# A hybrid mixer and sparse expert block: expert weights split in units per block, down product in f16, block columns copied by GpSimd

## The reference

```python
p_sel, g_sel = lax.top_k(p_group, 1)                 # group of a token
top_logits, top_idx = lax.top_k(sel_logits, TOP_K)   # two experts in it
gates = (p_sel * jax.nn.softmax(top_logits, axis=-1)).reshape(-1)
...
def expert_block(args):
    xb, e = args
    h = jax.nn.silu(xb @ w_gate[e]) * (xb @ w_up[e])  # w_gate, w_up: 1024 x 256
    return h @ w_down[e]                              # w_down: 256 x 1024
...
out = jnp.zeros((n + 1, d)).at[buf_tok].add(y * buf_gate[:, None])[:n]
```

## Time and profile before

| | us |
|---|---|
| median of 3 runs (lowest, highest) | 3261.25 (3260.13, 3263.42) |
| profiled execution, its own time | 3270.86 |
| its span, first to last instruction | 3269.3 |
| busy: PE, DVE, ACT, POOL | 3003.3, 2566.0, 2012.5, 949.9 |
| mean granted TensorE clock | 0.965 |

### The profile page before, as it was taken

The page is one execution under the profiler, slowest core; times in us unless marked ns, Lnnn a source line. Parts: engine busy times, 40 slices in busy tenths (PEclk is TensorE's granted clock), DMA queues, the critical chain, the costliest instruction groups (busy, mean ns, idle before and its releaser), DMA issues. The chain is left out here.

```text
span 3269.3 us, 82047 instructions
## 1 busy us (share of the span) xinstructions
PE 3003.3 (92%) x28810; PEld 2246.0 (69%) x28811; DVE 2566.0 (78%) x7193; ACT 2012.5 (62%) x4458; POOL 949.9 (29%) x994
## 2 busy tenths in 40 slices
PE   4878999999999999999999999997699999999970
PEld 4767878878887888788888878884344455554530
DVE  6678778887887888788878878886777888888755
ACT  7455566656565656665666656553566677777646
POOL 4213122212221322222122213222344444444420
PEclk9889999999999999999999999998899999999985
DMA  7010111121112121112112121115387777777749
GB/s 270 21 53 14 47 66 68 65 76 63 66 66 72 60 73 66 66 64 68 66 66 72 64 75 60 69 57 206 117 248 217 233 206 214 192 219 217 221 99 393
DMA packets 117811, 380.30 MB, mean 116 GB/s; under 512 B 18560, under 2 KB 18688, under 8 KB 105216
## 3 DMA queue, kind: packets, MB, share of 16 engines
q1 hardware_dynamic: 82528, 269.96, 22.8%
q0 software_dynamic: 29216, 89.30, 11.9%
q10 hardware_dynamic: 5760, 16.85, 1.3%
HBM read 280.05 MB, written 96.01 MB: 115 GB/s over the span
## 5 line engine op out<-in xcount | busy, mean ns | idle before, releaser
L597 PE MATMUL pj<-uT,W 128*128 128x128 f16 x15840 | 982.7, 220 | 8.1 <-POOL W L1732 8.1
L597 PEld LDWEIGHTS pj<-uT,W 128*128 128x128 f16 x15840 | 936.3, 98 | 54.1 <-issue 43.5
L2078 DVE SCALAR_TENSOR_TENSOR W<-W,ecol 128x512 f16<-128x512 f16 x664 | 447.4, 746 | 111.4 <-ACT W L2022 108.7
L2022 ACT ACTIVATE W<-W,ecol 128x512 f16 x664 | 415.8, 708 | 79.6 <-issue 77.3
L1986 PE MATMUL bA<-W,uT 128*128 128x512 f16 x1992 | 446.6, 381 | 5.4 <-issue 4.1
L1986 PEld LDWEIGHTS bA<-W,uT 128*128 128x128 f16 x1992 | 193.4, 98 | 229.0 <-issue 9.9
L1970 PE MATMUL pj<-W,qs 128*128 x664 | 303.3, 600 | 3.7 <-issue 2.8
L1781 POOL TENSOR_TENSOR dec<-tri,g 128x512 f32<-128x512 f32 x33 | 34.3, 1039 | 925.8 <-DVE g L1501 925.8
L953 ACT ACTIVATE ht<-ht 128x512 f32<-128x512 f32 x256 | 159.7, 625 | 87.5 <-DMA ht<-w_up 83.1
L1970 PEld LDWEIGHTS pj<-W,qs 128*128 128x128 f32 x664 | 121.4, 193 | 126.6 <-issue 126.3
L983 ACT ACTIVATE qh<-bA 128x256 f32<-128x256 f32 x198 | 76.6, 387 | 193.7 <-PE bA L697 189.7
(11 more groups left out here) (462 smaller groups left out, 6328.7 us busy)
## 6 DMA issues: line engine op xcount, KB each, us to landing
ht<-w_gate SPq DMA_DIRECT2D x128, 256.0 KB, 3.1
ht<-w_up SPq DMA_DIRECT2D x128, 256.0 KB, 3.3
W<-w_gate SPq DMA_DIRECT2D x32, 1024.0 KB
W<-w_up SPq DMA_DIRECT2D x32, 1024.0 KB
W<-w_down SPq DMA_DIRECT2D x32, 1024.0 KB
x_in<-xm SPq DMA_DIRECT2D x33, 512.0 KB, 4.4
ht<-xm SPq DMA_DIRECT2D x32, 512.0 KB, 3.5
h_rows<-ht SPq DMA_DIRECT2D x32, 512.0 KB
```

Of the source, the lines that this page charges most:

```text
L597: mm = pe.matmul(pj[g % 2][:, j, :], w16[:, k, w_half(w_high, COL[GROUPS[g]], 512, j * P, P)], (ul if low_u else uh)[:, k, :], start=(k == ...
L2022: nc.scalar.activation(part_of(wx[par][:, 0], k), raw[:, k], ACT.Copy, scale=ecol[par][:, k:k + 1]).then_inc(sem("wx_high"), 1)
L2078: a = nc.vector.scalar_tensor_tensor(out=part_of(wx[par][:, 1], k), in0=raw[:, k], scalar=ecol[par][:, k:k + 1], in1=part_of(wx[par][:, 0] ...
```

## The change

- The f16 halves of an expert's weights are now kept in one of two split rooms behind three raw slots, and include w_down. They are made ahead in units of half an expert: during block b the unit that `units_tab` names for it, of the next expert, is split (four chunks of gate/up, and one half of w_down, 1024 columns): `gu_high`, `down_high` on ScalarE, `gu_low`, `down_low` on VectorE. Each expert gets at least two blocks (`LEAST`). Blocks past the second split the second half again.
- VectorE scales the hidden rows by their largest value (`hidden`), they are turned and kept as two f16 halves (`hm16`), and the down product is twelve f16 matmuls in place of four f32 ones. Both output halves are written by ScalarE (`out_rows`) with the scale back.
- The squares of w_down are summed too: twelve chunks per expert in place of eight, placed one by one in ScalarE's order.
- The offsets of a block are read by one load of several words per engine and block.
- GpSimd copies the block's columns (`ecol`) in `ids`, and makes the gate column in `gates`.
- SyncE loads expert e when both units of expert e - 3 are split. Sigmoid times x becomes one Silu. The loop of `blocks` is compiled for 62 pairs (up to there, skipped ones included), where it was 46.

```diff
-WSLOTS = 4
+RAW_SLOTS = 3
+UNIT = 1024
+SQ = SLOT // 512
+NITER = P
+LEAST = 2
...
-                        raw_squares(s, 2, 3)
+                        raw_squares(s, 4, 5)
...
+                table_link(nc.vector.tensor_scalar(nb, nb, float(LEAST), None, ALU.max))
...
-            with eng.Fori(2, (NBLK - 2) // 2) as p:
+            with eng.Fori(2, (NITER - 4) // 2) as p:
...
+                for e in range(RAW_SLOTS, NE + 1):
+                    sp.wait_ge(sem(f"w_loaded{(e - 1) % RAW_SLOTS}"), 48 * ((e - 1) // RAW_SLOTS + 1))
+                    sp.sem_inc(sem("w_ready"), 2)
+                    if e < NE:
+                        split = sp.value_load(starti[0:1, e - RAW_SLOTS:e - RAW_SLOTS + 1], min_val=2, max_val=NITER)
+                        sp.wait_ge(sem("wd_low"), split)
+                        settle(sp)
+                        load_expert(sp, e, e % RAW_SLOTS)
...
                 def ids(b, par):
...
                     pool.dma_start(gid[par][:], idx_tab[bass.ds(off, P), :]).then_inc(sem(f"gid_in{par}"), 16)
+
+                    need(pool, sem("wd_low"), b + 1)
+                    settle(pool)
+                    nc.gpsimd.tensor_copy(ecol[par][:, 0:5].unsqueeze(1), half_rows[:, bass.ds(within(ahead, 3, 2 * NE), 1), 0:5])
+                    nc.gpsimd.tensor_copy(ecol[par][:, 5:7].unsqueeze(1), half_rows[:, bass.ds(within(now, 1, 2 * NE - 1), 1), 5:7]
+                                          ).then_inc(sem("ecol_ready"), 1)
+
+                def gates(b, par):
+
+                    pool.wait_ge(sem("ids_kept"), b + 1)
+                    pool.wait_ge(sem("ecol_ready"), b + 1)
+                    need(pool, sem("oc_ready"), b - 1)
+                    settle(pool)
+                    nc.gpsimd.tensor_tensor(gcol[par][:], gall[:, bass.ds(b, 1), 1:2].bitcast(F32).rearrange("p a c -> p (a c)"),
+                                            ecol[par][:, 6:7], ALU.mult).then_inc(sem("gate_in"), 1)
...
                 def body(b, par, last):
...
                     nc.gpsimd.tensor_copy(gall[:, bass.ds(b, 1), :], gid[par][:].unsqueeze(1)).then_inc(sem("ids_kept"), 1)
+                    gates(b, par)
                     if not last:
                         need(pool, sem(f"xg_in{1 - par}"), 8 * b + (0 if par == 0 else 8))
                         need(pool, sem("ids_kept"), b)
...
+                def down(b, w):
+                    pe.wait_ge(sem("hm_low"), b + 1)
+                    pe.wait_ge(sem("wd_low"), b + 2)
+                    need(pe, sem("yo_ready"), b)
                     for half in range(2):
...
+                        for part, h in ((1, 0), (0, 0), (0, 1)):
+                            for j in range(2):
+                                a = 2 * GU + 2 * UNIT * j + D * part + 512 * half
+                                mm = pe.matmul(flat(pj[half]), hm16[:, h, j, :], w[:, a:a + 512],
+                                               start=(j == 0 and part == 1), stop=(j == 1 and h == 1))
...
                 def body(b, par, last):
...
                     if not (isinstance(b, int) and b == 0):
-                        out_half(b - 1, 1 - par)
+                        out_rows(b - 1, 1 - par)
                     act.wait_ge(sem("hm_turned"), b + 1)
                     need(act, sem("y_full"), b + 1)
-                    nc.scalar.activation(hm2, bT[:, 0:2, :], ACT.Copy).then_inc(sem("hm2_ready"), 1)
+                    nc.scalar.activation(hm16[:, 0], bT[:, 0:2, :], ACT.Copy).then_inc(sem("hm_high"), 1)
+                    if not last:
+                        act.wait_ge(sem("y_full"), b + 1)
+                        down_high(*unit_of(raw, split), ecol[par][:, 4:5], range(1))
+                        split_ahead(b + 1, 1 - par, ready, unit_of(raw_ahead, split_next))
...
                 def body(b, par, last):
                     if isinstance(b, int) and b == 0:
...
+                        dve.wait_ge(sem("wx_high"), 2)
+                        gu_low(*first_unit, first_col, range(2))
+                        dve.wait_ge(sem("wd_high"), 2)
+                        down_low(*first_unit, first_col(0, 4), range(2))
                         turned(0)
...
+                    hidden(b, par)
                     if not last:
                         turned(b + 1)
...
+                    dve.wait_ge(sem("hm_high"), b + 1)
+                    nc.vector.tensor_tensor(hm16[:, 1], bT[:, 0:2, :], hm16[:, 0], ALU.subtract).then_inc(sem("hm_low"), 1)
+                    if not last:
+                        dve.wait_ge(sem("wd_high"), b + 3)
+                        down_low(*unit_of(raw, split), ecol[par][:, 4:5], range(1))
+                        dve.wait_ge(sem("wx_high"), b + 4)
+                        gu_low(*unit_of(raw_ahead, split_next), unit_col(1 - par), range(1))
```

More of the change, by code:

```diff
@@ L1705, in _ @@
+                expert, pos, half, odd, third = (tcol[:, n:n + 1] for n in (0, 1, 8, 9, 10))
+                idx_off, row, slot_off, next_row, raw_off, split_off = (tcol[:, n:n + 1] for n in range(2, 8))
                 table_link(nc.vector.tensor_scalar(ohb, end, iota_p[:], None, ALU.is_le))
-                table_link(nc.vector.tensor_reduce(tcol[:, 0:1], ohb, AX, ALU.add))
-                table_link(nc.vector.tensor_scalar(tcol[:, 0:1], tcol[:, 0:1], NE - 1.0, None, ALU.min))
-                table_link(nc.vector.tensor_scalar(ohb, iota_e[:], tcol[:, 0:1], None, ALU.is_equal))
@@ new lines, in _ @@
+                table_link(nc.vector.tensor_tensor_reduce(nb, ohb, start, 1.0, 0.0, ALU.mult, ALU.add, pos))
+                nc.vector.tensor_scalar(odd, expert, 0.5, -0.25, ALU.mult, ALU.add)
+                nc.vector.tensor_scalar(third, expert, 1.0 / RAW_SLOTS, None, ALU.mult)
+                table_link(nc.vector.tensor_tensor(pos, iota_p[:], pos, ALU.subtract))
+                nc.vector.tensor_copy(tcoli[:, 0:1], odd)
+                nc.vector.tensor_copy(tcoli[:, 1:2], third)
+                table_link(nc.vector.tensor_scalar(pos, pos, float(TCAP // P), float(P), ALU.min, ALU.mult))
@@ new lines, in _ @@
+                nc.vector.tensor_copy(odd, tcoli[:, 0:1])
+                nc.vector.tensor_copy(third, tcoli[:, 1:2])
+                nc.vector.tensor_scalar(half, pos, 8.0, float(UNIT), ALU.mult, ALU.min)
+                table_link(nc.vector.scalar_tensor_tensor(out=idx_off, in0=expert, scalar=float(TCAP), in1=pos,
+                                                          op0=ALU.mult, op1=ALU.add))
+                nc.vector.tensor_scalar(row, expert, 2.0, 1.0, ALU.mult, ALU.add)
+                nc.vector.tensor_scalar(next_row, expert, 1.0, NE - 1.0, ALU.add, ALU.min)
@@ L1862, in blocks, with within, loaded, unit_of @@
             return stop
[L1864 to L1874 removed]
+        def within(value, low, high):
+            return nc.s_assert_within(value, low, high)
+        def loaded(eng, words):
+            _, values = nc.values_load_multi_w_load_instructions(words, engines=[eng.engine], min_val=0,
+                                                                 max_val=2 * (RAW_SLOTS + 1) * SLOT + 2 * UNIT)
+            return values
+        def unit_of(raw, split):
+            raw = within(raw, 0, (RAW_SLOTS - 1) * SLOT + UNIT)
+            split = within(split, 2 * RAW_SLOTS * SLOT, 2 * (RAW_SLOTS + 1) * SLOT + 2 * UNIT)
+            return W[:, bass.ds(raw, SLOT - UNIT)], W16[:, bass.ds(split, 2 * (SLOT - UNIT))]
+        first_unit = W[:, 0:SLOT], W16[:, 2 * RAW_SLOTS * SLOT:2 * (RAW_SLOTS + 1) * SLOT]
+        def unit_col(par):
+            return lambda half, k: ecol[par][:, k:k + 1]
+        def raw_gu(unit, half, k):
+            return unit[:, 0:GU].rearrange("p (g k f) -> p k g f", g=2, f=FE)[:, 4 * half + k]
+        def split_gu(unit, half, part, k):
+            a = 2 * GU // 2 * part + 512 * (4 * half + k)
+            return unit[:, a:a + 512].rearrange("p (g f) -> p g f", g=2)
+        def raw_down(unit, half):
+            return unit[:, GU + UNIT * half:GU + UNIT * half + D]
+        def split_down(unit, half, part):
+            a = 2 * GU + 2 * UNIT * half + D * part
+            return unit[:, a:a + D]
+        def first_col(half, k):
+            return etab[:, 0, half, k:k + 1]
         def gathers(b, par):
@@ L2035, in body @@
                     if isinstance(b, int) and b == 0:
-                        high_part(0, 0)
+                        act.wait_ge(sem("w_ready"), 2)
+                        gu_high(*first_unit, first_col, range(2))
+                        down_high(*first_unit, first_col(0, 4), range(2))
                         x_part(0)
-                    if not last:
-                        high_part(b + 1, 1 - par)
+                        ready, raw, split = loaded(act, units_tab[:, 0:3])
+                        split_ahead(0, 0, ready, unit_of(raw, split))
@@ L2107, in body @@
+                        dve.wait_ge(sem("wx_high"), 3)
+                        gu_low(*unit_of(raw, split), unit_col(0), range(1))
```

(7 more changed lines are left out.)

310 lines of the change are left out of this document (164 added, 146 removed).

## The result

The changed kernel took 4297.3 us (median of 4 runs, 4293.3 to 4300.6); the kernel before, run beside it, 3262.0 us. The ratio is 1.317 [1.316, 1.319]: nearly a third slower. The forecast was 4230, with a range of 3900 to 4470.

What follows compares the result with a forecast made beforehand. TensorE, 97% busy in the expert stage, was taken as the bound before; afterwards GpSimd's wait delaying gathers. Profiled 3270.86 + 925 (blocks) + 9 (start) + 10 (skipped turns) + 25 (router) = 4240, less 9.6 for the median: 4230, range 3900 to 4470.

Steps and rivals of the forecast that it cites:

- The mechanism: Expert stage: GpSimd's column copies wait for VectorE's low down part, holding back the next gather; 21.1 us a block; chance 0.88.
- down product to gather's issue: Expert stage: output rows, hidden-row copy, high and low down parts, GpSimd copies and add before the gather: 7.1 us.
- landing, nothing beside it: Expert stage: gather from issue to TensorE's turn, with the add in its queue but no expert load: 6.5 us.
- turn and down product: TensorE, expert stage: turn of x and f16 down product, 3.5 us warm plus 2.1 lost to low clock: 5.6 us.
- skipped turns: Block loop compiled for 62 turns: 15 more skipped at 0.69 us each, 10 us in all (0 to 15).
- router stage: Router stage: four more chunks of squares per step delay one hand-over, 0.6 us a step: 25 us with preamble (0 to 80).
- start of the expert stage: Before the first block: the first gather waits for the first unit to be split, 12.2 us against 3.2: +9 us.
- The signs: Expert-stage trace: TensorE waits 6 to 9 us per block; blocks 19 to 21 us apart, 24 to 27 with a load.
- Rival B: Expert stage: gathers stay ahead; a ring of ScalarE and VectorE binds at 10.3 us a block, near 3330; chance 0.06.
- Rival C: Expert stage: neither ring binds, TensorE's saved work decides: 3215 us, 1.4% faster; chance 0.05.
- Rival D: Expert stage: same wait, cheaper: 16.8 us a block, 3850; its mirror 25.8, 4620; within the forecast's chance of 0.88.
- Rival E: Weight splitting: code splits 85 units, not 64; no effect while the gather wait binds; no chance given.

Runs made afterwards that it cites:

- columns_last: Changed kernel with GpSimd's wait for VectorE's low down part, column copies and gate column moved to the end of its body, next gather right behind: 3430.6 us.
- loop_of_46: Changed kernel with the block loop compiled for 46 pairs instead of 62, so 5 turns are skipped and not 21: 4285.8 us, one run.
- adds_before_ids: Changed kernel with GpSimd's add and kept ids moved ahead of the id step, so the gather follows the column copies at once: 4070.6 us, one run.
- scalar_load_first: columns_last with ScalarE's load of the unit offsets (six words) moved to the head of its body, ahead of its wait for gate/up: 3400.4 us.
- three_edits: scalar_load_first with TensorE turning hidden rows at the head of its next body, behind its offset load, and the loop compiled for 46 pairs: 3336.5 us.

## Why the prediction was right, point by point

The mechanism was the one named, and columns_last shows it: a reordering on GpSimd alone takes 867 of the 1035 us away. That the sum fell so near is in part luck, as the terms show:

| term | predicted | measured |
|---|---|---|
| down product to gather's issue | 7.1 | 8.6 or 9.0, mean 8.9 |
| landing, nothing beside it | 6.5 | 5.2 to 6.5, mostly 5.75 |
| landing beside a load (29 of 84) | 12 | 8.5 to 10.45, mostly 9.7 |
| turn and down product | 5.6 | 5.1 to 6.2, mean 5.7 |
| round, mean | 21.1 | 21.7 |
| skipped turns | +10 | +8.8 in the idle time, 11.5 in loop_of_46 |
| router stage | +25 | +38.4 |
| start of the expert stage | +9 | +18.1 (56.5 - 38.4) |

- *The chain's issue part* was 1.8 us short in the mean and 1.5 in the round shown. There ScalarE's and VectorE's steps are nearly as worked out (to 3015.64, 4.55 us for 4.1 predicted). What I had at 0.1 are GpSimd's steps: 0.49 us from VectorE's end to the first copy, 0.17 between the copies, 0.80 ahead of the add. The rows that I had read of the kernel before showed gaps of 0.17 on GpSimd.
- *The landing* was 1.3 us too long in the mean (0.655 x 5.75 + 0.345 x 9.7 = 7.1 for 8.4). With the add out of the way it was 4.5 us (adds_before_ids), near the 4.4 of the first gather of the earlier trace rows, so the add in the same queue costs some 1.25 us and not the 2.1 I took.
- These two errors mostly cancel, by luck and not by working. The forecast is 67 us low. Of that the expert stage with its skipped turns is 40, and the router stage and start 22; another 6 come from taking the profiled execution to be 9.6 us above the median, where it was 3.3. The sum was closer than its parts.
- *The signs.* Blocks were 19.9 to 21.0 us apart, and 24.0 to 24.9 where an expert was loading, as named. The wait at TensorE's turn of x was named at 6 to 9 us and read at 8.4 to 10.1, and at 13.0 to 13.7 beside a load. The forecast's own terms give 7.1 + 6.5 - 5.7 = 7.9 us and, beside a load, 13.4: the sign left the loads out, and the rest is the longer issue part.
- *Router stage.* The place of the delay was seen, its size was not. TensorE's waits for ScalarE's copies there grew from 2.9 to 8.5 us (L724) and from 0.7 to 6.5 us (L791, 29 times); a second hand-over is late in nearly every step, which my one step at chunk 3 did not have. In the first 230 us, the preamble, a wait grew by 6 us (L907, 24.5 to 30.4), near the 5 I gave it. The rest of the 38 was not traced.
- *Start.* The first gather was issued at 2362.43, 51.6 us later than in the earlier trace rows, and turned after 9.35 us, against 4.4 there; I had moved the issue, by 9 us, and not the landing.
- *Low clock.* 5.6 us for turn and down product: 1.97 and mostly 3.6 to 4.3 were read, overlapping by 0.2.
- *Rival B* (gathers ahead, 3330) had a true shape and a wrong size: columns_last, in which the gathers are ahead, is 3431. Most of the missing part is the offset loads, which that ring's sum did not hold: 0.38 us a block on ScalarE (scalar_load_first) and 0.6 on TensorE, with the loop's branch (three_edits, 52 / 84). With both moved away and without the loop's edit (11.5) the kernel would be, as an estimate, at 3348.
- *Rival C* (TensorE decides, 3215) did not come about even with the gathers ahead. A down product at the high clock did fall from 3.6 to 2.75 us, and the kernel became slower all the same. The Trainium skill (Perfetto Trace Analysis, Identifying the Most-Contended Engine) sends one to the engine with the highest occupancy first, but the same section calls the busy share of matmuls no good measure of how near TensorE is to its limit, and looks at the share of its weight loads among others instead. By that share TensorE was at 50% before (413.78 of 830 us) and not at 97, which my use of the page left out. Neither share shows the 10.5 us by which GpSimd's gathers were ahead, and that lead decided here.
- *Rival D's* low end is added wrongly: its own terms, 1421 us for the stage and the same 44 for the rest, give 3873 and not 3850.
- *Rival E* holds as a reading of the code (VectorE split 340 chunks, four for each of 85 units), and it did not matter while the gathers bound.
- *The DMA estimate.* The Trainium skill (DMA: Bandwidth & Descriptors, the section on the anatomy of one SWDGE DMA) gives 3.2 us for such a gather. The shortest read is 4.2 us (adds_before_ids), the usual one 5.75 behind an add and 9.7 beside a load, each from the gather's issue to TensorE's turn, so the measurement decides against it.

## What to carry to other kernels

Before moving work to an engine that is mostly idle, list what is queued behind it there and how far ahead that queue runs. Here the queue that prefetched could not take a wait on the block's results, however short the work behind the wait: with 0.4 us of copies and one 0.2 us product ahead of the next gather the kernel took 867 us more than with them last in the body. And when one tie is undone, look at the same queue again before blaming the work: here the second tie stood right behind the first.

## What was not expected of the hardware

- Loads of a few words into registers are not small. Between the high half of x and the output rows ScalarE stood 1.97 us for six words, and 4.6 us for nine with their bound checks; on TensorE a load of two words, with the loop's branch, stood 1.0 us ahead of gate/up in the mean and 2.3 at most (80 us in 79 blocks). What such a load costs hangs on where it stands: moved to the head of ScalarE's body, the load of six words gave back 30 us, 0.36 a block, of the 0.5 by which it had outlasted the down product.
- From its issue to TensorE's turn a gather of 512 KB took 4.5 us alone, 5.75 with an accumulating add issued 2.3 to 2.5 us ahead of it, and 9.7 beside a 3 MB load.
- A turn of the loop that is skipped cost 0.72 us of the kernel's time in the mean (16 turns, 11.5 us, one run).
